# Gate and up projections of a decoder FFN: two column tiles at a time by Strassen's scheme

## What is computed

```
hn = rms_norm(x, norm2_g)
gt, up = jnp.split(hn @ w_gu, 2, axis=-1)
return x + (jax.nn.silu(gt) * up) @ w_down
```

## Time and profile before

| what | us |
|---|---|
| median of 3 runs | 1944.82 |
| lowest and highest of them | 1942.38, 2065.7 |
| the profiled execution, its own time | 1947.0 |
| its span | 1945.2 |
| PE busy | 1854.0 (95%) |
| POOL, DVE, ACT busy | 700.7, 770.6, 632.5 |

### The profile page before, as it was taken

How to read it: one execution, slowest core, us unless ns; L and a number is a source line. 1 busy time by engine, 2 the same in 40 slices (tenths; PEclk the granted TensorE clock), 3 DMA queues, 4 the chain that set the end, 5 groups by cost and what they waited for, 6 DMA issues and landing times.

```text
span 1945.2 us, 33977 instructions
## 1 busy us (share of the span) xinstructions
PE 1854.0 (95%) x13982; PEld 1780.1 (92%) x13982; DVE 770.6 (40%) x1534; ACT 632.5 (33%) x1079; POOL 700.7 (36%) x376
## 2 busy tenths in 40 slices
PE   7988999999999999999999899989999999999999
PEld 6977888899999999999999778878899999999998
DVE  4645775235322212212425558642353221222232
ACT  4333214555432222212333322236543321222122
POOL 2313442433333434434333233425133334344342
PEclk8989999999999999999999999999999999999999
DMA  5222125211222232222223222241022222322222
GB/s 145 76 70 57 51 73 138 60 44 55 88 76 85 82 87 79 85 85 76 79 77 76 55 71 65 70 131 55 23 77 87 76 83 82 86 78 85 82 74 90
DMA packets 285700, 151.47 MB, mean 78 GB/s; under 512 B 17830, under 2 KB 284138, under 8 KB 285546
## 3 DMA queue, kind: packets, MB, share of 16 engines
q1 hardware_dynamic: 285546, 149.30, 27.3%
HBM read 141.89 MB, written 7.37 MB: 77 GB/s over the span
## 4 chain that ended last, share of the span: by engine, by line
PE 78%; DVE 11%; issue 3%; ACT 3%; SPq 2%; POOL 2%; DMA 1%; DVEq 0%; ACTq 0%; POOLq 0%
PE prod L1119 68%; PE aux L1488 2%; DVE scores L2293 1%; POOL w_lo L1520 1%; DVE top L2291 1%; PE aux L1189 1%; PE aux L1478 1%; SPq L959 1%; DVE in_lo L1939 1%; SPq L965 1%; PE aux L1250 1%; PE aux L1452 1%; DMA x_rows<-in_x_sample 1%; DVE qiz L2237 1%; PE aux L1134 1%
## 5 line engine op out<-in xcount | busy, mean ns | idle before, releaser
L1520 POOL TENSOR_TENSOR w_lo<-w_raw,w_hi 128x1024 fp32r<-128x1024 f32 (+1 forms) x246 | 598.6, 2433 | 1147.5 <-ACT w_hi L1613 1140.0
L1119 PE MATMUL prod<-in_hi,w_hi 128*128 128x288 f32 x2912 | 650.0, 305 | 12.8 <-DVE in_lo L2080 5.0
L1119 PE MATMUL prod<-in_lo,w_hi 128*128 128x288 f32 x2912 | 627.3, 297 | 0.0
L1119 PE MATMUL prod<-in_hi,w_lo 128*128 128x288 f32 x2912 | 627.2, 297 | 0.0
L1119 PEld LDWEIGHTS prod<-in_hi,w_hi 128*128 128x128 f32 x2912 | 470.0, 191 | 30.6 <-issue 18.8
L1119 PEld LDWEIGHTS prod<-in_lo,w_hi 128*128 128x128 f32 x2912 | 472.7, 190 | 0.0
L1119 PEld LDWEIGHTS prod<-in_hi,w_lo 128*128 128x128 f32 x2912 | 472.7, 190 | 0.0
L1613 ACT ACTIVATE w_hi<-w_raw 128x1024 fp32r<-128x1024 f32 (+1 forms) x246 | 254.8, 1036 | 273.7 <-PE prod L1119 273.7
L1119 PE MATMUL prod<-mid_hi,w_hi 128*128 128x288 f32 x960 | 207.7, 298 | 3.5 <-POOL w_lo L1520 3.4
L1119 PE MATMUL prod<-mid_hi,w_lo 128*128 128x288 f32 x960 | 206.4, 296 | 0.0
L1119 PE MATMUL prod<-mid_lo,w_hi 128*128 128x288 f32 x960 | 206.3, 296 | 0.0
(11 more groups left out here) (276 smaller groups left out, 1598.0 us busy)
## 6 DMA issues: line engine op xcount, KB each, us to landing
w_raw<-in_w_ffn_gu SPq DMA_DIRECT2D x88, 512.0 KB, 3.8
w_raw<-in_w_in SPq DMA_DIRECT2D x76, 512.0 KB, 3.8
w_raw<-in_w_ffn_down SPq DMA_DIRECT2D x32, 512.0 KB, 3.9
w_raw<-in_w_o SPq DMA_DIRECT2D x16, 512.0 KB, 4.0
w_raw<-in_w_ffn_down SPq DMA_DIRECT2D x16, 384.0 KB, 3.4
k_pages<-in_cache_k SPq DMA_DIRECT2D x32, 128.0 KB, 2.1
v_pages<-in_cache_v SPq DMA_DIRECT2D x32, 128.0 KB, 2.0
w_raw<-in_w_ob SPq DMA_DIRECT2D x16, 256.0 KB, 2.9
```

The costliest lines, as they stand in the source:

```text
L1119: ins = e.matmul(slot(g)[:, h, :], w[:, slot_w, i * P:(i + 1) * P], a[:, i, h * HALF:(h + 1) * HALF], start=first, stop=last)
L1520: e.tensor_tensor(w_lo[:, p % 2, 0:n], w_raw[:, p % RAW_RING, 0:n], w_hi[:, p % 2, 0:n].bitcast(F32), ALU.subtract).then_inc(w_lo_done, 1)
```

## The change

The gate and up panels go from the list of panels. In their place, for each of the 22 pairs b (gate tile b and up tile b), seven products P1 to P7 are made. The matrix of weights is read as 2 x 2 blocks: rows 0-511 and 512-1023 of the contraction by gate and up; the tokens as two halves of 288. So each product is four 128-row steps, 288 columns, 3 matmuls a step: 12 matmuls into one bank of `aux`.

- **Weights.** SP loads gate and up tile b into `ff_raw` (two pairs deep). DVE makes four sums of 128 x 512 from them (`fsum`: S1, S2, S4, S3). ACT copies each product's 128 x 512 weight to `ff_hi`, POOL subtracts for `ff_lo` (`fprep`). The ring has 4 slots; the split of product q+4 follows product q.
- **Activations.** After each `o` panel ACT and DVE also make the four sums and differences of the normed tiles and their high parts and remainders (`t_sum`, `t_hi`, `t_lo`; steps `turned`, `turned_low`); after `o` panel 3 the first four weight sums, after `o` panel 5 the split for the first four products.
- **Results.** PSUM goes on accumulating: P1, then P6 and P7 and P4 are added in the same bank (`fA`), P5 and P3 in another (`fB`), P2 in a third (`fC`). After P1, P5, P6 and P7 ACT copies the running sum to SBUF (`fcopy`, 128 x 288); the next product into that bank waits for that copy. DVE puts gate and up together in halves from copies and banks (`fsum_low`, `fgate`, `fup`, `fmid`), with `fgated` as L2039 and L2042 before, `flow` as L1939.
- **Order.** P1, P5, P2 of a part's first tile; then for each tile P6, P3, next P1, P7, next P2, next P5, P4. At a part's last tile the first steps of `down` panel 0 stand where the next tile's products would.
- `rstd` of norm 2 is made after P3 of tile 0, in a bank of `prod`.

```
+def ff_products():
+    order, first = [], 0
+    for n in FF_PARTS:
+        order += [("P1", first), ("P5", first), ("P2", first)]
+        for b in range(first, first + n):
+            more = b + 1 < first + n
+            order += [("P6", b), ("P3", b)] + ([("P1", b + 1)] if more else []) + [("P7", b)]
+            order += ([("P2", b + 1), ("P5", b + 1)] if more else []) + [("P4", b)]
+        first += n
+    return order
+FF_ORDER = ff_products()
+FF_PLACE = {name: i for i, name in enumerate(FF_ORDER)}
+FF_COPIED = [x for x in FF_ORDER if x[0] in ("P1", "P5", "P6", "P7")]
+FF_SUMS = [(s, b) for b in range(FF_TILES) for s in ("S1", "S2", "S4", "S3")]
+FF_SUM_OF = {"P5": "S1", "P6": "S2", "P7": "S3", "P3": "S4"}
+FF_SLOTS = 4
...
+    def product(self, name, b):
+        if name == "P1":
+            self.open(("fA", b), b % 2, 0)
+        if name == "P5":
+            self.open(("fB", b), 2, 0)
+        if name == "P2":
+            self.open(("fC", b), 3, 0)
+        self.add("fprod", name, b)
+        if name in ("P1", "P5", "P6", "P7"):
+            self.add("fcopy", name, b)
+        ahead = FF_PLACE[name, b] + FF_SLOTS
+        if ahead < len(FF_ORDER):
+            self.prepare(*FF_ORDER[ahead])
+    def prepare(self, name, b):
+        self.add("fprep", name, b)
+        if name == "P4" and b + 2 < FF_TILES:
+            self.add("fload", "up", b + 2)
...
+        self.product("P1", first)
+        self.product("P5", first)
+        self.product("P2", first)
+        self.add("fsum_low", first)
+        down = first_down
+        early = [2, 2] if n == 8 else [1, 2]
+        done = 0
+        for b in range(first, first + n):
+            more = b + 1 < first + n
+            self.product("P6", b)
+            self.ff_sums(b + 1, ("S1",))
+            if b > first:
+                self.add("flow", b - 1)
+            self.ff_sums(b + 1, ("S2",))
+            self.product("P3", b)
+            if part == 0 and b == 0:
+                self.rstd(2)
+            self.add("fgate", b)
+            if more:
+                self.product("P1", b + 1)
+            else:
+                self.start(down)
+                for i in range(early[0]):
+                    self.add("part", down, i)
+                done = early[0]
+            self.n_gated += 1
+            self.gate_tmp(("gate", b), "gate_used", self.n_gated)
+            self.add("fsigmoid", b)
+            self.ff_sums(b + 1, ("S4", "S3"))
+            if b + 2 < FF_TILES:
+                self.add("fload", "gate", b + 2)
+            self.product("P7", b)
+            self.add("fgated", b)
+            if more:
+                self.product("P2", b + 1)
+            else:
+                for i in range(done, done + early[1]):
+                    self.add("part", down, i)
+                done += early[1]
+            self.add("fup", b)
+            if more:
+                self.add("fsum_low", b + 1)
+                self.product("P5", b + 1)
+            self.product("P4", b)
+            self.split(("ff", b))
+            self.add("fmid", b)
+        self.add("flow", first + n - 1)
...
+                self.add("turned", idx)
                 self.stat(2, idx)
+                self.add("turned_low", idx)
+                if idx == 3:
+                    self.ff_sums(0, ("S1", "S2", "S4", "S3"))
+                if idx == 5:
+                    for name in FF_ORDER[0:FF_SLOTS]:
+                        self.prepare(*name)
...
+                        if b < 2 and which == "gate":
+                            e.wait_ge(ready(("o", 3)), filled(("o", 3)))
+                        if b >= 2 and which == "gate":
+                            e.wait_ge(ff_summed, ff_sum_no("S3", b - 2) + 1)
+                            e.wait_ge(ff_lo_done, ff_no("P2", b - 2) + 1)
+                        if b >= 2 and which == "up":
+                            e.wait_ge(ff_lo_done, ff_no("P4", b - 2) + 1)
...
+                        before = {"P6": "P1", "P3": "P5", "P7": "P6", "P4": "P7"}[name]
+                        e.wait_ge(ff_copied, ff_copy_no(before, b) + 1)
+                    e.wait_ge(ff_lo_done, q + 1)
+                    for k in range(4):
...
+                        e.matmul(out, ff_hi[:, q % FF_SLOTS, w], hi, start=first, stop=False, skip_group_check=True)
+                        e.matmul(out, ff_hi[:, q % FF_SLOTS, w], lo, start=False, stop=False, skip_group_check=True)
+                        ins = e.matmul(out, ff_lo[:, q % FF_SLOTS, w], hi, start=False, stop=(k == 3),
+                                       skip_group_check=True)
+                    ins.then_inc(ff_done, 1)
...
+                        e.tensor_tensor(ff_lo[:, q % FF_SLOTS, :], ff_weights(name, b),
+                                        ff_hi[:, q % FF_SLOTS, :].bitcast(F32), ALU.subtract).then_inc(ff_lo_done, 1)
...
+                        if q >= FF_SLOTS:
+                            e.wait_ge(ff_done, q - FF_SLOTS + 1)
+                        if name in FF_SUM_OF:
+                            e.wait_ge(ff_summed, ff_sum_no(FF_SUM_OF[name], b) + 1)
+                        else:
+                            e.wait_ge(ff_raw_ready[b % 2][int(name == "P4")], 16 * (nth(b, FF_TILES) // 2 + 1))
+                        e.activation(ff_hi[:, q % FF_SLOTS, :], ff_weights(name, b), ACT.Copy).then_inc(ff_hi_done, 1)
+                    elif kind == "fcopy":
+                        _, name, b = step
+                        e.wait_ge(ff_done, ff_no(name, b) + 1)
+                        e.activation(ff_kept(name, b), aux[:, bank(ff_bank(name, b)), 0:HALF],
+                                     ACT.Copy).then_inc(ff_copied, 1)
...
+                        x, y, op = {"S1": (up[:, lower], up[:, upper], ALU.add),
+                                    "S2": (ff_sum[:, 0, :], gate[:, lower], ALU.subtract),
+                                    "S3": (gate[:, lower], up[:, lower], ALU.subtract),
+                                    "S4": (gate[:, upper], ff_sum[:, 1, :], ALU.subtract)}[name]
+                        e.tensor_tensor(out, x, y, op).then_inc(ff_summed, 1)
...
+                        e.tensor_tensor(tmp[:, v, 0:HALF], ff_kept("P1", b), aux[:, bank(key), 0:HALF],
+                                        ALU.add).then_inc(free(key), 1)
...
+                        e.tensor_tensor(tmp[:, v, HALF:NT], ff_kept("P6", b), aux[:, bank(key), 0:HALF],
+                                        ALU.add).then_inc(free(key), 1)
+                        e.wait_ge(free(("fC", b)), emptied(("fC", b)))
+                        e.wait_ge(free(key), emptied(key))
+                        e.tensor_tensor(tmp[:, v, :], tmp[:, v, :], rstd[:], ALU.mult).then_inc(ff_gate_in, 1)
...
+                        both = ff_kept("P5", b)
+                        e.wait_ge(ff_copied, ff_copy_no("P7", b) + 1)
+                        e.tensor_tensor(both, both, ff_kept("P7", b), ALU.add).then_inc(dve_step, 1)
+                        e.wait_ge(dve_step, turn(dve_step))
+                        e.tensor_tensor(tmp[:, v, HALF:NT], tmp[:, v, HALF:NT], both, ALU.mult).then_inc(ff_mid_in, 1)
...
+                        if norm == 2 and kt >= 4:
+                            e.wait_ge(t_lo_done, t_no(1, k) + 1)
+                            e.scalar_tensor_tensor(out=t_sum[:, 1, k, :], in0=x2, scalar=scale, in1=t_sum[:, 1, k, :],
+                                                   op0=ALU.mult, op1=ALU.add).then_inc(t_summed, 1)
+                            e.scalar_tensor_tensor(out=t_sum[:, 2, k, :], in0=x2, scalar=scale,
+                                                   in1=in_sum[:, 0, k, HALF:NT], op0=ALU.mult,
+                                                   op1=ALU.subtract).then_inc(t_summed, 1)
+                            e.wait_ge(t_summed, t_no(2, k) + 1)
+                            e.scalar_tensor_tensor(out=t_sum[:, 3, k, :], in0=x1, scalar=scale, in1=t_sum[:, 1, k, :],
+                                                   op0=ALU.mult, op1=ALU.subtract).then_inc(t_summed, 1)
```

More of the change, by code:

```diff
@@ L176, in make_panels @@
     for part, n in enumerate(FF_PARTS):
-        for i in range(first, first + n):
-            out.append(("gate", (part, i), [("w_ffn_gu", 0, KD, i * P, P, 0)]))
-            out.append(("up", (part, i), [("w_ffn_gu", 0, KD, D_FF + i * P, P, 0)]))
         for m in range(KD):
@@ L439, in build_layer @@
         self.add("mix", "attention")
+        for b in range(2):
+            self.add("fload", "gate", b)
+            self.add("fload", "up", b)
         for p in range(first["oab"], base + N_LAYER):
@@ L442, in build_layer @@
             last_part = kind == "down" and idx[0] == len(FF_PARTS) - 1
-            self.start(p)
-            for i in range(KD):
+            done = 0
+            if kind == "down" and idx[1] == 0:
+                done = self.ff_part(idx[0], base, p)
+            else:
+                self.start(p)
+            for i in range(done, KD):
```

(6 more changed lines are left out.)

274 lines of the change are left out of this document (227 added, 47 removed).

## The result

The changed kernel takes 2062.26 us (median of 4; 2060.66 to 2064.23) against 1943.6 (median of 4) before: ratio 1.0617, 95% interval 1.0597 to 1.0638, so **6.2% slower**, beyond the predicted range of 1935 to 2020. (One of the four executions before, 2065.7, fell in a slower state of the chip, and the ratio goes by the other three, median 1942.38.) The time is 38 us over the 2024 that rival C gave for T = 15. It is only 11 over the 2051 of C's last case, but that case has T = 15.7, which was not measured, and the rest comes from the `o` panels and the parts' ends: this nearness is chance.

A forecast was written before the change was run, and what follows sets the result against it. PE's matmuls bound the FFN before, turns between DVE and POOL after. FFN +17.4, `o` panels +15.8, `rstd` -4.2 make +29.0 on the profiled 1947.0; less 2.2 to the median, 1973.8, about 1974 us; range 1935 to 2020.

The forecast's parts named there:

- rival C: Gate/up pairs: DVE's in-order queue is the bound, from T = 14.2; 2024 us at T = 15; chance 0.27.
- T: Time of one gate/up pair after the change; forecast 12.7 to 14.3 us, taken as 13.7.
- C's last case: Gate/up pairs: if the port is held for the whole of each instruction, T is 15.7 us, the kernel 2051.
- POOL's and DVE's exclusion: Gate/up pairs: operations with both DVE inputs in SBUF take turns with POOL's; each POOL operation can hold DVE 0.95 us.
- The stall at `rstd`: Start of the gate/up pairs: four products in the ring remove PE's 2.1 us stall a layer, -4.2 in all.
- I take T = 13.7: Gate/up pairs: chosen pair time in us, nearer to the DVE queue's sum of 13.5 than to the high end.
- 8.2 + 6.7 - 1.4: DVE's queue per pair: own work, plus holds by seven POOL operations, less what three PSUM operations cover: 13.5 us.
- so are the loads, with the same bytes: Gate/up weight loads: claimed hidden behind other work, since the bytes are the same; no cost counted.
- the prediction's own formula: FFN per layer: 136r + 24.25 with r = T/7; 290.4 us against 281.7 before, +8.7.
- +0.3, +0.3, +1.0: Ends of the three FFN parts: us added because few `down` steps cover the last `fmid`, `mid_hi` and `flow`.
- 7.9 together: `o` panels: us added a layer by activation work and first splits ahead of the panels' weights; 15.8 in all.
- The term for panel 7: `o` panel 7: four splits ahead of its weights make them late, 11.7 against 6.4, so 5.3 us a layer.

The follow-up runs named there:

- e3: On e1, the ten DVE operations of a pair with both inputs in SBUF cut to 8 columns, leaving work out; 1897.24 us, ratio 0.9759.
- e5: On e1, POOL's subtractions cut from 512 to 8 columns after a layer's first four, DVE whole; 1898.04 us, ratio 0.9765.
- e9: On e1, `rstd` and the sigmoid's result also put in PSUM as inputs of three 576-column DVE operations, nothing left out; 1955.39 us, ratio 1.0053.
- e1: Changed kernel with the gate tile of pair b+3, not b+2, loaded after sums S4 and S3 of pair b+1; 2049.26 us, ratio 1.0541.
- e2: Changed kernel with the ten DVE operations of a pair with both inputs in SBUF cut to 8 columns, loads unchanged; 1966.19 us, ratio 1.0114.
- e15: e9 without e1's edit: inputs in PSUM, but the gate tile loaded as in the changed kernel; 2028.12 us, ratio 1.043.
- e7: On e1, at a part's end sums S4 and S3 and the gate load for the next part moved behind `flow`; 2047.63 us, ratio 1.0535.
- e12: e9 and e7 together, plus `o`-phase work reordered, P3 and P6 remainders on DVE, `down` panel 1's weights split after the last P4; 1945.39 us, ratio 1.0006.
- e14: e9 plus e12's parts' ends alone: next part's sums and the split of `down` panel 1's weights moved later; 1946.36 us, ratio 1.0008.

## Why the prediction was wrong

**Right.** 528 matmuls are gone, and 12 matmuls into one bank keep their pace: 84 take 11.16 us, 0.133 each, where 11.21 was forecast. POOL's and DVE's exclusion, read from two overlaps in the earlier trace rows, is there in e3, e5 and e9, and the turn is of the size forecast: 0.76 plus 0.95 is 1.71, measured 1.745. The stall at `rstd` is gone, -2.1 a layer. Of the rivals C named the bound, DVE's queue; only the place where ACT stands is `mid_hi` and not `fsigmoid`. The direction, slower, was that of the forecast too; what failed are four terms of its sum.

**The step "I take T = 13.7".** The sum for DVE's queue was 8.2 + 6.7 - 1.4, the last term for three operations with a PSUM input, which were to run under POOL's subtractions at no cost. In e1 the pair is 14.7: 8.1 + 7 x 0.95 = 14.75, as if there were no credit. Two of the three PSUM operations (810.03 and 810.40) run while POOL stands idle from 809.80 to 812.46, because ACT stands at `mid_hi` and hands it no copy: they lie just ahead of what ACT waits for, and so in the one gap where POOL has nothing to do. The third (813.07) does run under a subtraction, and the operation behind it waits 0.52 instead of about 1.0. The other six waits of a pair are 0.95 to 1.1 each, so seven times 0.95 is a mean and its exactness is luck; measured are 6.7 us of waits where 5.3 were forecast. C's reason, that DVE's waits don't fall together with POOL's turns, is near to this, and its threshold (over 14.2) is met. A pair's time is 38.9 us a microsecond: 1.0 from 13.7 to 14.7 is 39 us.

**The step "so are the loads, with the same bytes" (hidden, at nothing).** Bytes were the same, but not the place. Before, a panel's weight had a slot of its own; now a slot of `ff_raw` is free only when the last product of its pair is split, SP issues in order, and the later of two loads at once lands 5.6 to 6.6 us after the first was issued (five such twos from 590 to 660 us), where one alone takes 3.8. The loop alone is 13.3 to 13.6 a pair (e2). On top of the port it costs 13 us (e1), with the port eased 72.7 (e15 against e9). It is the second of two bounds of nearly one height, and no rival had it. By the pairs it brings T from 14.7 to 15.1.

**With T = 15.0,** near the 15.1 measured from the third pair of a part on, the prediction's own formula gives +33.9 - 1.6 = +32.3 a layer for the pairs; measured +31.0, for the first two pairs of a part are shorter. So the model of the pairs was right but for T.

**The step "+0.3, +0.3, +1.0" for the parts' ends.** Measured +16.5 a layer with the `down` panels. The step took 2 to 3 us for the last `fmid`, `mid_hi` and `flow`; but at that point DVE is behind by its backlog. PE waits 5.57, 5.58 and 0.85 us for the last `mid_lo`, ahead of the last step of `down` panel 0 in each of the three parts. After the two long waits it runs at 0.50, for 11 matmuls (689.19 to 692.0, see the stretches above) and for 22 (860.72 to 866.1), which costs 1.4 and 2.5 us. The waits are 12.0 of the 16.5, the half clock 3.9. That the backlog's tail is no constant but hangs on DVE's and POOL's next work shows in e7, and in e12 to e14, where no single wait there is over 2.0.

**The step "7.9 together" for the `o` panels.** Measured 13.5. The term for panel 7 held (4.48, forecast 5.3). The waits of the panels ahead of it are 5.2, of which 0.7 was there before, where 2.6 was forecast; and the half clock behind the two longest waits, 2.3 and 1.6 us, was not in the sum at all. 8.9 of added waits and 3.9 are 12.8; the other 0.7 was not traced.

The four rows add up: the forecast had pairs 23.9 too low, ends 14.9, `o` phase 5.6, `rstd` 0, together 44.4 a layer or 88.8; the forecast 1973.8 and these give 2062.6, against 2062.26. That it is so near is in part chance: the spans of the profiled executions differ by 114.8, the two layers' stretches by 118.3, and the 3.5 us that come back in the other stages were not traced.

**Left open.** A third slot of `ff_raw` was not tried, nor is the half clock separated from the waits that go ahead of it; in the pairs too PE runs at the lower clock at times (granted 0.96 to 0.97 over the parts), and what that adds to T is not shown. Whether DVE's queue at 11.96 a pair could go to PE's 11.16 by an order of its operations that lets POOL run under the PSUM ones was not tried either.

## What to carry to other kernels

A matmul saved is paid in element work on other engines: before it is counted as gained, take the queue of each of them with its waits, not its busy share (DVE at 60% of the span was the bound). Where two engines take turns, a turn costs most of the other's instruction (0.95 to 1.1 of 1.27 us here), and a credit for what runs "under" it holds only if the other is then at work; a common input held in PSUM took three operations out of the turns and 2.7 us off each pair. When a ring is freed by the last of many readers and a queue issues in order, the loop from that reader over the load to the first user has to be added up like an engine, for it can hide behind another bound and show its price (13 or 73 us) only when that is gone.
